# Eight slots for the first modulation weights, and the input's squares summed over tiles by TensorE

## The chip, the core and the metric

The kernel runs on one core of a Trainium2 chip. A core has TensorE (PE in the profile; its weight loads are PEld), VectorE (DVE), ScalarE (ACT) and GpSimd (POOL), and SyncE (SP), which here does nothing but issue transfers. The engines run their own instruction lists and meet only at semaphores. The metric is the device time of one execution in microseconds, less is better.

## The reference

The program computes two transformer blocks on one sequence of 512 tokens and 1024 features, in float32. What the change touches is the very first step of the first block:

```
mod = einsum('bd,de->be', silu(c), w_ada) + b_ada        # 1024 x 6144 weights
shift1, scale1, gate1, shift2, scale2, gate2 = split(mod, 6)
y    = x * rsqrt(mean(x * x, axis=-1) + eps)             # per token, over 1024 features
hmix = (y * g_norm1) * (1 + scale1) + shift1
proj = hmix @ w_in                                       # 1024 x 11264 weights
```

After it come stick-breaking attention, retention, a gated feed-forward layer, and the second block with a gated delta rule, a long convolution, cross attention and another feed-forward layer. Of all six parts of `mod` only `shift1` and `scale1` are needed before the first large product can start.

## The kernel before

Activations lie with features on the 128 partitions: `resid` is x as 8 tiles of 128 features by 512 tokens. Large products are done in three TensorE passes, on a high and a low part of each operand, so each weight unit (128 x 1024, 512 KB, tile `raw`) is split: ScalarE writes `w_hi` (`split_hi`), GpSimd then writes `w_lo` = raw - w_hi (`split_lo`, L449), and TensorE waits for both. There are 324 such units in a ring of four slots. Every engine's order is written out by hand, one function per engine, and no scheduler moves anything.

The opening stage, before the first large product, runs like this.

- SyncE issues the three constant tables, then 16 blocks of modulation weights (`ada0`, 512 KB each; blocks 0 to 7 give `shift1`, 8 to 15 `scale1`), with `resid` (2 MB) behind block 3, then the first weight units. `ada0` has four slots, so from block 4 on each issue waits until VectorE has used the block four places earlier (L382 to L386).
- VectorE multiplies each block by the activated conditioning vector and accumulates over 8 blocks in `adac0` (`ada`, L975 for a first block, L976 for the others). Between blocks 13 and 14 stands `invert()` (L981), the reciprocal of the norm's root, which waits for ScalarE's root. Behind block 15 stand the addition of the bias (L993), the gain (L995) and the normalised tiles (`tn` L1008, `x_lo` L1004).
- ScalarE squares the 8 tiles of `resid` (`square_tile`), the first into `sqacc`, the others into the two halves of `tn`; GpSimd adds each to `sqacc` (`add_square`, L436). ScalarE then waits for the sums over features, takes the root, and only then splits the first three weight units (`w_hi`).
- TensorE sums over the partitions by multiplying with a column of ones. `modulation` (L1683) does this for the 8 column blocks of `adac0`; `stat` (`column_sums`, L1655) does it for `sqacc`, in four matmuls of one output column each, and `spread_rs` (L1662) broadcasts the reciprocal root over the partitions. Its order here is: modulation of blocks 0 to 7, stat, spread, modulation of blocks 8 to 15, first large product.

The profile has two records for each of these float32 matmuls: the four of `stat` are eight rows of L1655.

Of the kernel before, what the change touches and what calls it, by code (L numbers as in the profile page):

```python
# [33 lines left out]
F32 = mybir.dt.float32  # L34
# [3 lines left out]
ACT = mybir.ActivationFunctionType  # L38
AX = mybir.AxisListType

P = 128
D = 1024
KT = D // P
T = 512
NB = T // P
EPS = 1e-6
UNIT = 1024
RING = 4
AHEAD = RING - 1

SB_DIM = 64
PAIRS = 8
# [117 lines left out]
T0, _ = starts(TILES)  # L170
# [29 lines left out]
def build_program(nc, dram):  # L200
    ctx = ExitStack()
    with ctx:
# [42 lines left out]
        over = at[0]  # L245

        def overlay(start, *specs):

            out, o = [], start
            for name, shape, dt in specs:  # L250
                t, o = put(name, shape, dt, where=o)
                out.append(t)
            assert o <= nc.sbuf_usable_end, (specs, o - nc.sbuf_usable_end)
            return out, o

        gate_t = tn

        (ada0, adac0), _ = overlay(over, ("ada0", (P, 4, UNIT), F32), ("adac0", (P, 2, UNIT), F32))


        qk_at = [norm_at, norm_at + T * 4, norm_at + 2 * T * 4, norm_at + 3 * T * 4]
# [67 lines left out]
        def sem(name):  # L329
# [6 lines left out]

            "dve_step", "act_step", "pool_step",
            "decay_free", "decay_loaded", "consts_loaded", "x_loaded", "tables_loaded", "consts_ready", "stored",
            "ada0_loaded0", "ada0_loaded1", "ada0_loaded2", "ada0_loaded3", "ada1_loaded", "ada_used",
            "ada_ready", "c_ready_act",  # L340
            "sq_ready", "stat_ready", "root_ready", "recip_ready", "rs_ready", "res_ready", "rsq_ready", "rsq_used",
            "hs_ready", "hrecip_ready", "glogit_ready", "tap_ready", "tap_used", "normed", "norm_hi", "x_ready",
# [22 lines left out]
        @block.sync  # L365
        def _(sp_):
            def load(u):
                s = u.slot(RING)
                if u.i is not None or u.c >= RING:

                    sp_.wait_ge(lo_ready, (u + (1 - RING)).val())
                if u.i is None:
                    src = dram["weights"][u.c]
                else:
                    src = dram["weights"][bass.ds(u.val(), 1), :, :].rearrange("a p n -> (a p) n")
                sp_.dma_start(raw[s][:], src).then_inc(raw_loaded[s], 16)

            sp_.dma_start(cols[:], dram["cols"]).then_inc(S["consts_loaded"], 16)
            sp_.dma_start(small[:], dram["small"]).then_inc(S["consts_loaded"], 16)
            sp_.dma_start(halves[:], dram["halves"]).then_inc(S["consts_loaded"], 16)  # L380
            for n in range(16):
                if n >= 4:  # L382
                    sp_.wait_ge(S["ada_used"], n - 3)
                sp_.dma_start(ada0[:, n % 4, :], dram["ada"][n]).then_inc(S[f"ada0_loaded{n % 4}"], 16)
                if n == 3:
                    sp_.dma_start(resid[:], dram["x"]).then_inc(S["x_loaded"], 16)  # L386
            for u in range(RING):
                load(At(u))
            def load_units(first, end):
                with sp_.Fori(0, (end - first) // 4) as i:  # L390
                    for j in range(4):
                        load(At(first + j, i, 4))

            load_units(RING, U0["sb_out"] + 4)

            sp_.wait_ge(S["osb_ready"], PAIRS)
            sp_.dma_start(angles[:], dram["tables"][:, 0:2 * T]).then_inc(S["tables_loaded"], 16)
            load_units(U0["sb_out"] + 4, U0["ret"])
            with sp_.Fori(0, RET_H) as i:
                for j in range(16):  # L400
                    if 6 <= j < 14:

                        n = At(2 * KT + j - 6, i, 8)
                        sp_.wait_ge(S["ada_used"], n.val())
                        sp_.dma_start(ada1[:], dram["ada"][bass.ds(n.val(), 1), :, :]
                                      .rearrange("a p n -> (a p) n")).then_inc(S["ada1_loaded"], 16)
                    load(At(U0["ret"] + j, i, 16))
                    if j == 3:

                        sp_.wait_ge(S["decay_free"], i + 1)  # L410
                        sp_.dma_start(decay[:], dram["tables"][:, bass.ds(i * T + 2 * T, T)]
                                      ).then_inc(S["decay_loaded"], 16)
            rest = U0["ret"] + 64
            load_units(rest, U0["mix_out"] + 4)

            sp_.wait_ge(S["gdn_over"], 1)
            sp_.wait_ge(S["x_ready"], X_MIX)
            sp_.dma_start(memf[:], dram["mem"]).then_inc(S["mem_loaded"], 16)
            load_units(U0["mix_out"] + 4, NU)

            for k in range(KT):
                sp_.wait_ge(S["resid_ready"], k + 1)
                sp_.dma_start(dram["out"][:, k, :], resid[:, k, :]).then_inc(S["stored"], 16)
            sp_.wait_ge(S["stored"], 16 * KT)


        @block.gpsimd
        def _(pool):
            step = Count(pool, S["pool_step"])
            rsq, used = Count(pool, S["rsq_ready"]), Count(pool, S["rsq_used"])  # L430

            def add_square(k):

                rsq.next()
                if k:
                    used.own(nc.gpsimd.tensor_tensor(sqacc[:], sqacc[:], tn[:, k % 2, :], ALU.add))  # L436
                if k == KT - 1:
                    pool.sem_inc(S["sq_ready"], 1)

            def add_squares():  # L440
                for k in range(KT):
                    add_square(k)

            add_squares()

            def split_lo(u):
                s = u.slot(RING)
                pool.wait_ge(hi_ready, (u + 1).val())
                nc.gpsimd.tensor_tensor(w_lo[s][:], raw[s][:], w_hi[s][:].bitcast(F32),  # L449
                                        ALU.subtract).then_inc(lo_ready, 1)  # L450

            def split_units(first, end):
                with pool.Fori(0, (end - first) // RING) as i:
                    for j in range(RING):
                        split_lo(At(first + j, i, RING))

            split_units(0, U0["gdn_in"])

            def next_phase(first, end):

                for j in range(AHEAD):
                    split_lo(At(first + j))
                add_squares()
                split_lo(At(first + AHEAD))
                split_units(first + RING, end)

            next_phase(U0["gdn_in"], U0["mix_out"])

            tap_used = Count(pool, S["tap_used"])
            for m, (n, j) in enumerate(POOL_TAPS):  # L470
                if j:
                    pool.wait_ge(S["tap_ready"], m + 1)
                    tap_used.own(nc.gpsimd.tensor_tensor(cfy[:, n, :], cfy[:, n, :], tn[:, tap_used.at.c % 2, :],  # L473
                                                         ALU.add))
            pool.sem_inc(S["cf_pool"], 1)
            split_units(U0["mix_out"], U0["kv"])
            for j in range(AHEAD):
                split_lo(At(U0["kv"] + j))
            for k in range(KT):
                split_lo(At(U0["kv"] + AHEAD + k))  # L480
                if k:
                    add_square(k - 1)
            split_lo(At(U0["kv"] + AHEAD + KT))
            add_square(KT - 1)
            split_units(U0["kv"] + AHEAD + KT + 1, U0["up"])
            next_phase(U0["up"], NU)
# [3 lines left out]
        def _(act):  # L490
# [27 lines left out]
            def square_tile(k):  # L518

                if k >= 3:  # L520
                    own["rsq_used"].next()
                own["rsq_ready"].own(f(tn[:, k % 2, :] if k else sqacc[:], resid[:, k, :], ACT.Square))
# [14 lines left out]
            own["c_ready_act"].own(f(c_act[:], cols[:, C0["c"]:C0["c"] + KT], ACT.Silu))  # L537
            act.wait_ge(S["x_loaded"], 16)
            for k in range(KT):
                square_tile(k)  # L540
            own["rsq_used"].next(2)
            own["consts_ready"].next(6)
            root(1.0 / D)
            for u in range(AHEAD):
# [391 lines left out]
        def _(dve):  # L936
# [34 lines left out]
            def ada(w, dst, k):  # L971

                c = c_act[:, k:k + 1]
                if k == 0:
                    return V.tensor_scalar(dst[:], w, c, None, ALU.mult)  # L975
                return V.scalar_tensor_tensor(dst[:], w, c, dst[:], ALU.mult, ALU.add)  # L976
# [7 lines left out]
            for m in range(2):  # L984
                for k in range(KT):
                    n = m * KT + k
                    dve.wait_ge(S[f"ada0_loaded{n % 4}"], 16 * (n // 4 + 1))
                    own["ada_used"].own(ada(ada0[:, n % 4, :], adac0[:, m, :], k))
                    if n == 2 * KT - 3:
                        invert()  # L990

            own["ada_ready"].next(2)
# [589 lines left out]
        def _(pe):  # L1582
# [101 lines left out]
                ins.then_inc(S["ada_ready"], 1)  # L1684

            pe.wait_ge(S["consts_loaded"], 48)
            own["ada_used"].next(KT)
            modulation(adac0[:, 0, :])
            stat()
            spread_rs()  # L1690
            own["ada_used"].next(KT)
            modulation(adac0[:, 1, :], 1)
# [591 lines left out]
```

## Time and profile before

| What | us |
|---|---|
| Three timed runs, median (lowest to highest) | 2405.63 (2405.4 to 2406.29) |
| Profiled execution, span | 2403.4 |
| First large product starts, in the profiled execution | 49.72 |
| TensorE busy | 2154.4 (90%) |
| VectorE busy | 1154.8 (48%) |
| ScalarE busy | 881.3 (37%) |
| GpSimd busy | 949.1 (39%) |

The page gives the profiled execution's time as its span, from the first instruction to the last; the timed runs are 2.2 us longer at the median, which is what lies around the span. In a row of the timeline stand the start, the duration, the engine, the line and operation, what it writes and reads, how many instructions are merged in the row, and in brackets how long the engine had been idle and who released it. A merged row's duration runs from the start of its first instruction to the end of its last. In the page's chain of waits the end of the program is followed back from instruction to instruction.

### The profile page before, as it was taken

The page shows a single profiled execution, that of the slowest core. Times are in us where ns is not written, and L with a number is a line of the kernel's source. Part 1 is how long each engine was busy: PE and PEld are TensorE (multiplying, and loading weights), DVE is VectorE, ACT ScalarE, POOL GpSimd, SP SyncE. Part 2 cuts the span into 40 slices and gives each one's busy share as a digit, 9 for nine tenths or more (in the row PEclk, how much of TensorE's full clock was granted, in tenths as well). Part 3 has the DMA queues.
Part 4 walks back from the last instruction along what each step waited for, and adds up shares of the span by engine and source line. Part 5 has one row for each costly group of instructions (what it writes and reads, how often), then busy time and mean ns, then how long its engine had stood idle before and what let it go on. Part 6 is the DMA issues. An engine that isn't in the chain of part 4 may idle for free.

```text
span 2403.4 us, 28555 instructions
## 1 busy us (share of the span) xinstructions
PE 2154.4 (90%) x10018; PEld 1750.0 (73%) x10018; DVE 1154.8 (48%) x1216; ACT 881.3 (37%) x1027; POOL 949.1 (39%) x426
## 2 busy tenths in 40 slices
PE   3999998999999998999998899667979878888997
PEld 3778877787877877888886677656768556666785
DVE  6054402354454555111113743897671478787613
ACT  3466632323232334444223444543342333333321
POOL 3321133243433343444444433664275134334441
PEclk9999999999999998999999999898899999999998
DMA  7211032342424222322231221000233012222331
GB/s 250 88 38 50 9 123 102 117 150 99 157 83 148 70 91 70 102 96 96 97 105 61 79 79 62 1 1 1 97 99 129 22 49 84 74 87 71 101 108 44
DMA packets 56225, 203.58 MB, mean 85 GB/s; under 512 B 6240, under 2 KB 6368, under 8 KB 55904
## 3 DMA queue, kind: packets, MB, share of 16 engines
q1 hardware_dynamic: 56160, 202.70, 25.0%
q8 instruction: 43, 0.70, 0.1%
q14 instruction: 22, 0.18, 0.0%
HBM read 200.57 MB, written 2.10 MB: 84 GB/s over the span
## 4 chain that ended last, share of the span: by engine, by line
PE 66%; DVE 24%; ACT 3%; issue 3%; DMA 1%; POOL 1%; DVEq 1%; SPq 0%; ACTq 0%; POOLq 0%
PE acc L1598 16%; PE acc L1600 16%; PE acc L1599 16%; DVE tn L1558 5%; DVE cfy L1344 2%; PE aux L1598 2%; PE aux L1599 2%; PE aux L1600 2%; DVE tn L1293 2%; DVE tn L1556 2%; PE acc L1801 1%; PE aux L1655 1%; DVE fin L958 1%; DMA ada<-in_ada 1%; PE acc L1712 1%
## 5 line engine op out<-in xcount | busy, mean ns | idle before, releaser
L449 POOL TENSOR_TENSOR w_lo<-raw,w_hi 128x1024 fp32r<-128x1024 f32 x324 | 801.4, 2480 | 1299.3 <-ACT w_hi L495 1298.5
L1598 PE MATMUL acc<-x_hi,w_hi 128*128 128x512 f32 x1544 | 621.6, 403 | 68.5 <-DVEq L946 52.7
L1600 PE MATMUL acc<-x_hi,w_lo 128*128 128x512 f32 x1544 | 608.5, 394 | 0.0
L1599 PE MATMUL acc<-x_lo,w_hi 128*128 128x512 f32 x1544 | 608.4, 394 | 0.0
L495 ACT ACTIVATE w_hi<-raw 128x1024 fp32r<-128x1024 f32 x324 | 339.8, 1059 | 608.7 <-PE acc L1600 489.0
L1598 PEld LDWEIGHTS acc<-x_hi,w_hi 128*128 128x128 f32 x1544 | 294.5, 191 | 159.2 <-issue 78.5
L1600 PEld LDWEIGHTS acc<-x_hi,w_lo 128*128 128x128 f32 x1544 | 293.9, 190 | 63.3
L1599 PEld LDWEIGHTS acc<-x_lo,w_hi 128*128 128x128 f32 x1544 | 294.8, 191 | 58.2
L495 ACT ACT_TABLE_LOAD x91 | 116.8, 1283 | 53.0 <-PE aux L1655 22.7
L1558 DVE SCALAR_TENSOR_TENSOR tn<-fin,cols,tn 128x512 f32<-128x512 f32 x88 | 128.3, 1458 | 13.1 <-DVE tn L1558 3.3
L473 POOL TENSOR_TENSOR cfy<-cfy,tn 128x512 f32<-128x512 f32 x70 | 99.5, 1421 | 72.3 <-ACT tn L495 68.9
L1205 DVE TENSOR_TENSOR ht<-acc,tn 128x512 f32<-128x512 f32 x22 | 15.2, 691 | 182.5 <-PE acc L1600 178.7
L976 DVE SCALAR_TENSOR_TENSOR adac<-ada,c_act,adac 128x1024 f32<-128x1024 f32 x42 | 61.9, 1474 | 68.7 <-DMA ada<-in_ada 67.4
L1598 PE MATMUL aux<-w_hi,x_hi 128*128 128x512 f32 x192 | 76.2, 397 | 6.5 <-DVE x_lo L1004 5.2
L1599 PE MATMUL aux<-w_lo,x_hi 128*128 128x512 f32 x192 | 75.9, 395 | 0.0
L1600 PE MATMUL aux<-w_hi,x_lo 128*128 128x512 f32 x192 | 75.7, 394 | 0.0
L1598 PE MATMUL acc<-g_hi,w_hi 128*128 128x512 f32 x176 | 69.8, 396 | 0.2 <-DVEq L946 0.2
L1599 PE MATMUL acc<-g_lo,w_hi 128*128 128x512 f32 x176 | 69.7, 396 | 0.0
L1599 PE MATMUL acc<-h_lo,w_hi 128*128 128x512 f32 x176 | 69.7, 396 | 0.0
L1598 PE MATMUL acc<-h_hi,w_hi 128*128 128x512 f32 x176 | 69.7, 396 | 0.0
L1600 PE MATMUL acc<-g_hi,w_lo 128*128 128x512 f32 x176 | 69.7, 396 | 0.0
L1600 PE MATMUL acc<-h_hi,w_lo 128*128 128x512 f32 x176 | 69.7, 396 | 0.0
(320 smaller groups left out, 3335.7 us busy)
## 6 DMA issues: line engine op xcount, KB each, us to landing
raw<-in_weights SPq DMA_DIRECT2D x324, 512.0 KB, 3.5
ada<-in_ada SPq DMA_DIRECT2D x48, 512.0 KB, 3.7
resid<-in_x SPq DMA_DIRECT2D x1, 2048.0 KB, 12.5
out<-resid SPq DMA_DIRECT2D x8, 256.0 KB, 2.0
decay<-in_tables SPq DMA_DIRECT2D x4, 256.0 KB, 3.5
memf<-in_mem SPq DMA_DIRECT2D x1, 1024.0 KB, 4.8
angles<-in_tables SPq DMA_DIRECT2D x1, 512.0 KB, 3.6
small<-in_small SPq DMA_DIRECT2D x1, 320.0 KB, 3.1
```

The source lines that it names most:

```text
L449: nc.gpsimd.tensor_tensor(w_lo[s][:], raw[s][:], w_hi[s][:].bitcast(F32), ALU.subtract).then_inc(lo_ready, 1)
L473: tap_used.own(nc.gpsimd.tensor_tensor(cfy[:, n, :], cfy[:, n, :], tn[:, tap_used.at.c % 2, :], ALU.add))
L495: return nc.scalar.activation(out, in_, func, **kw)
L958: (end or step).own(V.tensor_tensor(dst, bank(t), rs_sb, ALU.mult))
L976: return V.scalar_tensor_tensor(dst[:], w, c, dst[:], ALU.mult, ALU.add)
L1293: ins = V.scalar_tensor_tensor(y, x, w, y, ALU.mult, ALU.add)
L1344: step.own(V.scalar_tensor_tensor(y, x, w, y, ALU.mult, ALU.add))
L1556: ins = V.tensor_scalar(y, x, w, b, ALU.mult, ALU.add)
L1558: ins = V.scalar_tensor_tensor(y, x, w, y, ALU.mult, ALU.add)
L1598: M(out, a_hi, b_hi, start=first, stop=False)
L1599: M(out, a_hi, b_lo, start=False, stop=False)
L1600: return M(out, a_lo, b_hi, start=False, stop=last)
```

## The change

It does three things. The ring for the first 16 blocks of modulation weights has eight slots instead of four, so an issue waits for the block eight places earlier. ScalarE writes the 8 squared tiles to 8 tiles of a new buffer `sq0`, with no wait between them but for its own writes, and signals once, behind the last; GpSimd's seven additions in this stage are gone, and `stat` sums over all 8 tiles, with 32 matmuls in place of 4, and now stands ahead of the first modulation in TensorE's list. And `invert()` stands behind block 8 in VectorE's list, not behind block 13. Later norms keep the old scheme.

```
-        (ada0, adac0), _ = overlay(over, ("ada0", (P, 4, UNIT), F32), ("adac0", (P, 2, UNIT), F32))
+        (ada0, adac0, sq0), _ = overlay(over, ("ada0", (P, ADA_RING, UNIT), F32), ("adac0", (P, 2, UNIT), F32),
+                                        ("sq0", (P, KT, T), F32))
...
             for n in range(16):
-                if n >= 4:
-                    sp_.wait_ge(S["ada_used"], n - 3)
-                sp_.dma_start(ada0[:, n % 4, :], dram["ada"][n]).then_inc(S[f"ada0_loaded{n % 4}"], 16)
+                if n >= ADA_RING:
+                    sp_.wait_ge(S["ada_used"], n - ADA_RING + 1)
+                sp_.dma_start(ada0[:, n % ADA_RING, :], dram["ada"][n]).then_inc(S[f"ada0_loaded{n % ADA_RING}"], 16)
...
-            add_squares()
...
             act.wait_ge(S["x_loaded"], 16)
             for k in range(KT):
-                square_tile(k)
-            own["rsq_used"].next(2)
+                (step if k < KT - 1 else own["sq_ready"]).own(f(sq0[:, k, :], resid[:, k, :], ACT.Square))
...
-                    dve.wait_ge(S[f"ada0_loaded{n % 4}"], 16 * (n // 4 + 1))
-                    own["ada_used"].own(ada(ada0[:, n % 4, :], adac0[:, m, :], k))
-                    if n == 2 * KT - 3:
+                    dve.wait_ge(S[f"ada0_loaded{n % ADA_RING}"], 16 * (n // ADA_RING + 1))
+                    own["ada_used"].own(ada(ada0[:, n % ADA_RING, :], adac0[:, m, :], k))
+                    if n == KT:
                         invert()
...
             pe.wait_ge(S["consts_loaded"], 48)
+            own["sq_ready"].next()
+            stat([sq0[:, k, :] for k in range(KT)])
             own["ada_used"].next(KT)
             modulation(adac0[:, 0, :])
-            stat()
             spread_rs()
```

On TensorE, from the start of its list to the first matmuls of the large product, the order before is this (`adac_83` is the buffer `adac0`).

```order
L1581 UNCONDITIONAL_BRANCH
L1683 MATMUL aux<-small,adac_83 128x1 x8
L1655 MATMUL aux<-small,sqacc 128x1 x4
L1662 MATMUL aux<-small,rcol 128x128 x4
L1683 MATMUL aux<-small,adac_83 128x1 x8
```

The same place in the changed kernel, whose lines are one less here, and in which `sq_84` is `sq0`:

```order
L1580 UNCONDITIONAL_BRANCH
L1654 MATMUL aux<-small,sq_84 128x1 x32
L1682 MATMUL aux<-small,adac_83 128x1 x8
L1661 MATMUL aux<-small,rcol 128x128 x4
L1682 MATMUL aux<-small,adac_83 128x1 x8
```

The sum of squares has moved to the front and has eight times the matmuls.

On VectorE, from the first modulation block to the gain, before (`ada_82` is `ada0`):

```order
L975 TENSOR_SCALAR adac_83<-ada_82,c_act 128x1024
L976 SCALAR_TENSOR_TENSOR adac_83<-ada_82,c_act,adac_83 128x1024 x7
L975 TENSOR_SCALAR adac_83<-ada_82,c_act 128x1024
L976 SCALAR_TENSOR_TENSOR adac_83<-ada_82,c_act,adac_83 128x1024 x5
L981 RECIPROCAL rcol<-rcol 128x4
L976 SCALAR_TENSOR_TENSOR adac_83<-ada_82,c_act,adac_83 128x1024 x2
L993 TENSOR_TENSOR mod<-aux,cols 128x16
L995 SCALAR_TENSOR_TENSOR gain_67<-mod,cols 128x8
```

and in the changed kernel:

```order
L974 TENSOR_SCALAR adac_83<-ada_82,c_act 128x1024
L975 SCALAR_TENSOR_TENSOR adac_83<-ada_82,c_act,adac_83 128x1024 x7
L974 TENSOR_SCALAR adac_83<-ada_82,c_act 128x1024
L980 RECIPROCAL rcol<-rcol 128x4
L975 SCALAR_TENSOR_TENSOR adac_83<-ada_82,c_act,adac_83 128x1024 x7
L992 TENSOR_TENSOR mod<-aux,cols 128x16
L994 SCALAR_TENSOR_TENSOR gain_67<-mod,cols 128x8
```

The reciprocal has moved up by five blocks: seven blocks now stand behind it, where two stood.

## Rows read from the trace of the kernel before

**Rows 1.** The page's first line.

```profile
span 2403.4 us, 28555 instructions
```

**Rows 2.** Chain of waits, first 57 us: start, duration, engine and work.

```profile
19.26 2.18 DVE adac L976
...
34.14 5.42 DMA ada<-in_ada
...
39.65 1.30 DVE adac L976
...
40.99 3.59 PE aux L1683 x16
...
44.88 1.86 DVE gain L995
...
48.37 1.21 DVE x_lo L1004
...
49.72 0.77 PE aux L1598
```

**Rows 3.** Windows: stretch, busy time by engine, granted TensorE clock, DMA share, GB/s.

```profile
15.00:20.00 5.00, 0.00 (x0) 0.00 (x0) 2.02 (x2) 1.89 (x3) 1.91 (x1) 1.00 0.98 399
20.00:25.00 5.00, 0.00 (x0) 0.00 (x0) 4.93 (x3) 1.42 (x3) 4.76 (x4) 1.00 0.83 238
```

**Rows 4.** Timeline of ScalarE in the opening stage.

```profile
16.65 0.63 ACT L495 ACTIVATE sqacc<-resid 128x512 f32<-128x512 f32 x1 [11.30 <-DMA resid<-in_x]
17.32 1.29 ACT L495 ACTIVATE tn<-resid 128x512 f32<-128x512 f32 x2
...
36.40 0.26 ACT L495 ACTIVATE rcol<-aux,eps 128x4 f32<-128x4 f32 x1
40.92 1.06 ACT L495 ACTIVATE w_hi<-raw 128x1024 fp32r<-128x1024 f32 x1 [4.25 <-DMA raw<-in_weights]
```

**Rows 5.** Timeline of TensorE in the opening stage.

```profile
25.98 3.54 PE L1683 MATMUL aux<-small,adac 128*128 128x1 f32 x16 [25.98 <-DVE adac L976]
33.14 1.87 PE L1655 MATMUL aux<-small,sqacc 128*128 128x1 f32 x8 [3.62 <-POOLq L438]
```

**Rows 6.** Timeline of TensorE, column sums between large products, at 1420 us.

```profile
1420.51 3.63 PE L1655 MATMUL aux<-small,kdec 128*128 128x1 f32 x32
1423.99 6.46 PE L1655 MATMUL aux<-small,vb 128*128 128x1 f32 x32
```

**Rows 7.** Windows of TensorE alone, same place: busy, granted clock, DMA share, GB/s.

```profile
1424.00:1427.00 3.00, 3.00 (x19) 0.59 0.51 169
1427.00:1430.00 3.00, 3.00 (x16) 0.50 0.06 25
```

**Rows 8.** Timeline of VectorE in the opening stage.

```profile
9.23 3.93 DVE L976 SCALAR_TENSOR_TENSOR adac<-ada,c_act,adac 128x1024 f32<-128x1024 f32 x3 [0.50 <-DMA ada<-in_ada]
...
36.79 0.18 DVE L981 RECIPROCAL rcol<-rcol 128x4 f32<-128x4 f32 x1
```

**Rows 9.** Timeline of GpSimd in the opening stage.

```profile
18.09 14.94 POOL L436 TENSOR_TENSOR sqacc<-sqacc,tn 128x512 f32<-128x512 f32 x7 [17.64 <-ACT tn L495]
42.05 6.97 POOL L449 TENSOR_TENSOR w_lo<-raw,w_hi 128x1024 fp32r<-128x1024 f32 x3 [9.02 <-ACT w_hi L495]
```

**Rows 10.** Timeline of VectorE and GpSimd in the second feed-forward layer, 2210 to 2225 us.

```profile
2210.56 0.75 DVE L1558 SCALAR_TENSOR_TENSOR tn<-fin,cols,tn 128x512 f32<-128x512 f32 x1 [0.15 <-DVE tn L1558]
...
2219.18 5.20 POOL L449 TENSOR_TENSOR w_lo<-raw,w_hi 128x1024 fp32r<-128x1024 f32 x2 [9.32 <-ACT w_hi L495]
2219.32 2.81 DVE L1558 SCALAR_TENSOR_TENSOR tn<-fin,cols,tn 128x512 f32<-128x512 f32 x1 [0.15 <-DVE tn L1556]
2222.29 2.65 DVE L1558 SCALAR_TENSOR_TENSOR tn<-fin,cols,tn 128x512 f32<-128x512 f32 x1 [0.15 <-DVE tn L1558]
```

**Rows 11.** Chain of waits, within the first large product.

```profile
50.49 0.43 PE aux L1599
...
55.99 0.24 PE aux L1600
```

More of the change, by code:

```diff
@@ L49 @@
 AHEAD = RING - 1
+ADA_RING = 8
 SB_DIM = 64
@@ L338, in build_program @@
             "decay_free", "decay_loaded", "consts_loaded", "x_loaded", "tables_loaded", "consts_ready", "stored",
-            "ada0_loaded0", "ada0_loaded1", "ada0_loaded2", "ada0_loaded3", "ada1_loaded", "ada_used",
+            *[f"ada0_loaded{n}" for n in range(ADA_RING)], "ada1_loaded", "ada_used",
             "ada_ready", "c_ready_act",
```

## The prediction

> **What bounds the kernel now.** I read the page first. Its span is 2403.4 us [rows 1], and the edited code all lies ahead of the first large product at 49.72 us [rows 2]. From there on TensorE goes its old way with the old instructions, so the question is how far that start moves. The second view is the chain of waits over the opening stage [rows 2]. It runs through VectorE's accumulation of the modulation blocks (`adac`). Each of them takes 2.18 us on the chain while GpSimd adds squares, 1.30 without. It then waits 5.42 us for the transfer of the last block, does that block at 39.65, and goes through TensorE's second modulation (3.59), the gain (1.86), the first `x_lo` (1.21) and into the product. The windows, third, show why the transfer was late: with the queue full the DMA moved 399 GB/s, with four slots tied to the slow VectorE 238 [rows 3]. So before, both VectorE beside GpSimd and the ring of four bind. The timelines of the engines, fourth, give the durations below.
>
> **Part 1, the eight slots.** With eight slots the issues are never behind VectorE: up to block 7 they wait for nothing, and block 15 waits for block 7. The bytes up to block 15 are 16 x 0.52 MB, 2.1 MB of `resid` and 0.8 MB of tables, 11.3 MB; at 399 GB/s that is 28 us, and with the 2 us before the first bytes all blocks are there by about 31 us, against 39.6. The first weight unit follows about 1.3 us later and the fourth at about 36. `resid` stands at the same place in the queue, so it lands as before, about 16.6; blocks 4 to 7 now queue right behind it. If they shared its engines a little it would be late by up to one block (1.3 us); I take 0 and keep 1.3 for the range.
>
> **Part 2, the squares.** ScalarE starts at 16.65; one square has a pitch of 0.67 us (16.65 to 17.32), so the eighth ends at 16.65 + 7 x 0.67 + 0.63 = 22.0 [rows 4]. GpSimd's 14.94 us of additions [rows 9] go, and with them the 0.9 us that each one added to a VectorE instruction beside it. But TensorE now has 32 matmuls, 64 records, where it had 8 records. In this stage 8 records take 1.87 us and 16 take 3.54 [rows 5], which is 0.21 us a record. So 64 take 1.87 + 56 x 0.21 = 13.6 us, and the sums are ready at 22.0 + 0.1 + 13.6 = 35.7. Before, they were ready at 33.14 + 1.87 = 35.01 [rows 5]. All that ScalarE gained is spent on TensorE, and 0.7 us more.
>
> Would the clock rise during 13.6 us of work? The granted-clock column reads 1.00 in these first windows, but the durations say otherwise. At 1420 us the same column sums come in two groups of 32 records behind large products [rows 6]. The first takes 3.63 us (0.11 a record) and the second 6.46 (0.20). The granted clock is 0.59 and then 0.50 in the second, 1.2 GHz, though TensorE is busy in all of it [rows 7]. The 0.21 of the opening is thus the lower level, and a stream of one-column matmuls did not hold the upper one, still less does it reach it. I cost all 64 records low. The Trainium skill, page "TensorE: Matmul & The Clock Gate", section "Part 1: The HAM clock gate", has sustained matmul activity raise TensorE from its lower to its full clock. By that rule alone the stream would speed up on its way; the trace does not agree for matmuls of this shape. It is a rival below.
>
> **Part 3, the reciprocal behind block 8.** This is the step that decides. VectorE's list is strict: the reciprocal waits for ScalarE's root, the root for the sums, and blocks 9 to 15 stand behind it. From the end of the sums to the end of the reciprocal it was 36.97 - 35.01 = 1.96 us [rows 5, 8]. So VectorE, done with block 8 at about 24.5 us, stands idle until 35.7 + 1.96 = 37.7, with all the data there from 31 on. Then come seven blocks at 3.93 / 3 = 1.31 each [rows 8], 9.2 us. Before, two stood behind it, and they waited for a transfer.
>
> Nor do they run alone. ScalarE splits the first weight unit when the root is done. The unit has landed by then, so this is at 36.66 + 0.7 = 37.4 instead of 40.92 [rows 4], and GpSimd starts `w_lo` at about 38.5, three in a row (before: 42.05 to 49.02, rows 9). What does one cost a block? In the feed-forward layer a VectorE instruction of this kind takes 0.75 alone and 2.81 and 2.65 beside two `w_lo` [rows 10], so each adds 1.9 to 2.1. In the opening a block of 1.28 to 1.30 took 2.18 beside an addition of half `w_lo`'s width, 0.9 more [rows 2, 9], 1.8 for the full width. I take 2.0 for each of three, 6.0 (bounds 5.4 and 6.6; zero if they didn't meet, a rival). Block 15 ends at 37.7 + 9.2 + 6.0 = 52.9, against 40.95.
>
> **Part 4, what is given back.** From block 15 to the large product it was 49.72 - 40.95 = 8.8 us [rows 2]. The gain took 1.86 because it stood beside a `w_lo`; the nearest instruction of that size alone is the reciprocal, 0.18 [rows 8], and the three `w_lo` are now over by about 49. That gives 1.7. The first `x_lo` took 1.21 and takes 0.75 alone, as in rows 10: 0.45. The rest stays, 6.6. The modulations keep their 3.54: the first one and the broadcast lie in VectorE's seven blocks and cost nothing while these last 15 us.
>
> **Sum.** The product starts at 52.9 + 6.6 = 59.5, which is 9.8 us later. As a check by differences: reciprocal 0.7 later, five more blocks behind it 6.6, the transfer wait of 1.4 us ahead of block 15 gone, contention 6.0, given back 2.1, makes +9.8. Afterwards the first matmuls go at 0.43 us and from 55.99 on at 0.24 [rows 11], as the clock rises 6 us after the start; should that fall earlier or later against the new start, by 2.5 us at most, it is worth -1.2 to +0.3. Nothing behind it absorbs a later start, since from there the chain is TensorE's own. The span becomes 2413.2, and with the 2.2 us that the median of the timed runs lies above the span, 2415.4.
>
> **Rivals.**
> 1. The clock rises from the first sums on (ends on the other side, no change). All 64 records at 0.11 are 7.3 us, the sums end at 29.4 and the reciprocal at 31.4. `w_hi` then waits for the first weight unit (about 32) and meets the blocks all the same. Block 15 ends at 31.4 + 9.2 + 6.0 = 46.6, the product starts at 53.2: +3.5, or +1.7 if the last modulation is fast too. 2407.3 to 2409.1. It decides from a record time of about 0.13 on; for it speaks only the length of the stream, against it rows 6 and 7.
> 2. The clock rises part way, after some 6 us as in rows 11: 28 slow records and 36 fast, sums at 32.1, +6.2, 2411.8. Slower still.
> 3. GpSimd's `w_lo` and the blocks don't hinder each other: 9.8 - 6.0 = +3.8, 2409.4, no change. Against it the 2.18 of rows 2 and the 2.65 of rows 10.
> 4. The start comes sooner, because VectorE does not stand still. With all blocks used as they land it would end block 15 at about 33 and the product would start at 40, 10 us sooner, 2396. This is what the eight slots would give by themselves; it needs the root by about 25 us, and the sums alone take longer.
>
> **How the numbers follow.** The forecast's own mechanism has 0.80, rival 2 has 0.06, rival 1 has 0.06, rival 3 has 0.05 and rival 4 with everything unforeseen on that side 0.03. A measurement of this kernel can tell about 0.2% from no change, 4.8 us. The forecast and rival 2 are slower, 0.86; rivals 1 and 3 are no change, 0.11; faster 0.03. The range of the forecast itself is +8 (contention at its low bound, an early clock) to +12 (at its high one, a late `resid`). To leave out no more than 2 in 10 it is stretched down to rivals 2 and, in part, 3: 2410 to 2418.
>
> **What would show it.** Right: TensorE's sums over `sq0` as one block of 64 records from about 22 to 36 us; VectorE idle from about 24.5 to 37.7, released by the root; three blocks of over 3 us beside `w_lo` and four of 1.3; the gain in about 0.2; the large product from about 59.5. Wrong: sums that end before 33, blocks of 1.3 beside `w_lo`, or a span that moves by less than the start of the product does, which would mean slack behind it that I don't see.

## The result and the profile after

| | median us | lowest to highest | runs |
|---|---|---|---|
| before | 2406.24 | 2405.4 to 2407.14 | 6 |
| changed | 2412.71 | 2410.44 to 2417.24 | 6 |

The ratio is 1.003, with a 95% interval of 1.0018 to 1.0041: slower by 7.2 us, 4.3 to 9.9. The forecast was 2415.4, its range 2410 to 2418. The profiled execution of the changed kernel has a span of 2410.9 us and took 2412.76. Two of the later runs, one in experiment 1 (3072 us) and one in 9 (4062 us), showed a much lower granted clock than all others (0.66 and 0.85), and the ratios leave them out.

This is the chain of waits of the changed kernel, first 65 us: start, duration, engine and work. It answers to [rows 2].

```profile
21.43 13.80 PE aux L1654 x64
...
36.61 0.27 ACT rcol L495
...
36.98 0.19 DVE rcol L980
37.19 1.30 DVE adac L975
38.51 3.27 DVE adac L975
41.81 3.25 DVE adac L975
45.09 3.26 DVE adac L975
48.37 1.30 DVE adac L975
...
52.35 3.59 PE aux L1682 x16
...
56.24 0.18 DVE gain L994
...
58.05 0.76 DVE x_lo L1003
...
58.95 0.76 PE aux L1597
...
63.12 0.43 PE aux L1597
63.55 0.30 PE aux L1598
63.85 0.23 PE aux L1599
```

Before, this chain ran through transfers and blocks. Now it waits for TensorE's sums, then for the root, and only then come seven blocks. Three of these take 3.26 us instead of 1.30. The large product starts at 58.95, 9.2 us later than the 49.72 of [rows 2]. Its matmuls reach their fast pace at 63.85, 4.9 us after the start; before, that took 6.3 us (55.99, rows 11). The matmuls are the same, and at 65 us the changed kernel is 8.5 us late instead of 9.2.

The timelines of the other three engines, of the changed kernel, answer to [rows 4, 8, 9].

```profile
16.03 5.26 ACT L495 ACTIVATE sq<-resid 128x512 f32<-128x512 f32 x8 [9.99 <-DMA resid<-in_x]
35.32 1.28 ACT L495 ACT_TABLE_LOAD   x1 [14.03 <-PE aux L1654]
```

```profile
22.60 0.75 DVE L974 TENSOR_SCALAR adac<-ada,c_act 128x1024 f32<-128x1024 f32 x1
36.98 0.18 DVE L980 RECIPROCAL rcol<-rcol 128x4 f32<-128x4 f32 x1 [13.63 <-ACT rcol L495]
37.19 15.10 DVE L975 SCALAR_TENSOR_TENSOR adac<-ada,c_act,adac 128x1024 f32<-128x1024 f32 x7
```

```profile
38.05 9.21 POOL L449 TENSOR_TENSOR w_lo<-raw,w_hi 128x1024 fp32r<-128x1024 f32 x3 [37.59 <-ACT w_hi L495]
```

The squares are done at 21.3, but the sums only at 35.2 (forecast: 22.0 and 35.7; before, the sums were ready at 35.01). VectorE stands idle for 13.63 us, released by ScalarE's root. Of the 1.93 us from the end of the sums to the end of the reciprocal, ScalarE's load of a function table ahead of the root is 1.28. Then GpSimd's three `w_lo` take 9.21 us where they took 6.97 [rows 9]. With no blocks beside them, in experiment 4, they take 6.96, so both sides pay.

These are windows of the changed kernel, with busy time by engine as in [rows 3]. The transfers run at full rate from 10 to 35 us, here from 25 to 35 (before: 238 GB/s from 20 us on, rows 3).

```profile
25.00:30.00 5.00, 5.00 (x25) 5.00 (x25) 0.00 (x0) 0.00 (x0) 0.00 (x0) 1.00 1.03 412
30.00:35.00 5.00, 5.00 (x25) 5.00 (x25) 0.00 (x0) 0.00 (x0) 0.00 (x0) 1.00 1.00 397
```

So the eight slots did their work, and VectorE (third busy column, 0.00) used none of it. The clock column reads 1.00 here although the records have the pace of the low clock: before the first change of clock in this trace, the column can't be relied on.

### The profile page after: what moved, and what is told of

It is laid out like the page before. It is cut to its first block, busy times and chain, and to the rows that moved or that the text cites. A ratio compares the mean times of both kernels' runs of the same rounds, so it can differ in the third digit from the quotient of the medians.

```text
span 2410.9 us, 28738 instructions
## 1 busy us (share of the span) xinstructions
PE 2166.1 (90%) x10074; PEld 1761.9 (73%) x10074; DVE 1153.2 (48%) x1216; ACT 881.1 (37%) x1027; POOL 937.8 (39%) x419
## 4 chain that ended last, share of the span: by engine, by line
PE 67%; DVE 23%; ACT 3%; issue 3%; POOL 1%; DVEq 1%; DMA 1%; SPq 0%; ACTq 0%; POOLq 0%
PE acc L1597 17%; PE acc L1599 16%; PE acc L1598 16%; DVE tn L1557 5%; DVE cfy L1343 2%; PE aux L1597 2%; PE aux L1598 2%; PE aux L1599 2%; DVE tn L1292 2%; PE aux L1654 2%; DVE tn L1555 2%; PE acc L1801 1%; DVE fin L957 1%; PE aux L1742 1%; PE acc L1712 1%
```

## The experiments

Each was profiled once and timed in up to five rounds beside the kernel before. The kernel before scattered by 9 to 16 us from its lowest to its highest time in these later runs, so medians are told with their ratio's interval. "Start" is the first matmul of the large product in the profile. "Square" is the start of ScalarE's first square, which waits for `resid`: it varies by 1.2 us between profiles, and by half a us between the two of the kernel before (16.65 and 17.20). That scatter is part of every start, so the text also counts starts "from the square", the difference of the two columns.

| kernel | start | square | median | before | ratio (95%) |
|---|---|---|---|---|---|
| changed | 58.95 | 16.03 | 2412.71 | 2406.24 | 1.0030 (1.0018 to 1.0041) |
| reciprocal behind block 13 | 49.36 | 16.54 | 2403.99 | 2406.38 | 0.9985 (0.9974 to 0.9995) |
| eight slots alone | 48.79 | 16.79 | 2404.29 | 2406.38 | 0.9991 (0.9982 to 0.9999) |
| squares alone, four slots | 48.47 | 17.18 | 2404.38 | 2406.38 | 0.9987 (0.9978 to 0.9997) |
| weight split after block 15 | 55.80 | 16.56 | 2410.78 | 2406.38 | 1.0016 (1.0007 to 1.0025) |
| sums tile by tile | 54.63 | 16.25 | 2409.91 | 2405.90 | 1.0009 (0.9998 to 1.0019) |
| reordered | 42.03 | 16.11 | 2397.45 | 2405.90 | 0.9957 (0.9945 to 0.9970) |
| clock raised ahead | 58.50 | 16.77 | 2412.49 | 2405.90 | 1.0026 (1.0014 to 1.0037) |
| one tile summed | 42.68 | 16.72 | 2398.51 | 2405.90 | 0.9965 (0.9952 to 0.9978) |
| before, again | 50.59 | 17.20 | 2406.81 | 2407.24 | 0.9998 (0.9988 to 1.0007) |
| start delayed | 58.15 | 17.20 | 2414.70 | 2407.24 | 1.0031 (1.0019 to 1.0044) |
| reordered, four slots | 46.96 | 17.05 | 2401.89 | 2407.24 | 0.9976 (0.9966 to 0.9987) |

**1. The reciprocal put back behind block 13.**

```
-                    if n == KT:
+                    if n == 2 * KT - 3:
                         invert()
```

> The changed kernel with the reciprocal put back behind block 13 of VectorE's list; all else as changed. Theory A (the place of the reciprocal decides: it stalls VectorE with seven blocks behind it, which then run into three w_lo): the sums still end at about 35.2 us and the reciprocal at 37.2, but only blocks 14 and 15 follow, one of them beside a w_lo, so block 15 ends at about 41.8 (changed: 52.3) and the large product starts at about 49.2 (changed: 58.95, before: 49.72). Time about that of before, 2405 to 2407. Theory B (the 32 matmuls of the sum are what costs, wherever the reciprocal stands): the start stays above 56 us and the time at 2410 or more.

Chain of waits of this kernel:

```profile
21.95 13.80 PE aux L1654 x64
...
37.71 1.30 DVE adac L975
39.03 3.27 DVE adac L975
...
42.34 3.58 PE aux L1682 x16
...
46.23 0.60 DVE gain L994
...
49.36 0.77 PE aux L1597
```

The sums are as long, and as late from the square, and the loss is gone: theory A. The place of one short instruction in VectorE's list is worth 9.6 us of start, 10.1 from the square. The median is 2.4 us under that of the kernel before, 1 us below the 2405 to 2407 that I expected.

**2. Eight slots alone.** (The kernel before, with `ADA_RING = 8` as in the change.)

> The kernel before with eight slots and nothing else changed. Theory A (the transfer wait of 1.4 us before block 15 goes, but the first w_lo now meets block 15): block 15 ends at about 41.6, the last w_lo at about 46.3, the product starts at about 49, 0.5 to 1 us sooner than before; 2405 to 2406, no difference that can be measured. Theory B (the transfer wait was the bound and all blocks move forward): blocks 4 to 15 at the pace of the transfers, the product starts before 46 and the time falls by 4 us or more.

Chain of waits of this kernel:

```profile
32.08 2.18 DVE adac L977
...
37.14 1.30 DVE adac L977
38.46 3.27 DVE adac L977
```

Theory A. The wait of 5.42 us for the last transfer is gone from the chain, but block 15 meets the first `w_lo` instead: the early weights start GpSimd early. The blocks up to 34 us still take 2.18 us beside GpSimd's additions. Start 48.79, 0.9 us sooner (1.1 from the square); the time is barely shorter.

**3. Squares on TensorE alone, four slots, reciprocal behind block 13.**

```
-ADA_RING = 8
+ADA_RING = 4
```

(and the edit of 1.)

> The changed kernel with four slots and the reciprocal behind block 13: only the squares are moved to TensorE. Theory A (the root binds, the slots are worth nothing here): blocks 4 to 13 run in about 1.3 us each and are done before the root, and the product starts as in the kernel with eight slots and the reciprocal behind block 13, about 49.2. Theory B (four slots starve VectorE also without GpSimd beside it): block 13 is not done by 37 us and the product starts 1 us or more later than with eight slots.

Start 48.47, not later than with eight slots in experiment 1: 0.9 us sooner, and 1.5 from the square. Block 13 ends at 33.9 us (30.8 with eight), both before the root. With four slots the weights come later, the first `w_lo` starts at 40.3 and meets no block: blocks 14 and 15 take 2.60 us together against 4.58 in experiment 1. So theory A, with a twist that I had not foreseen: the slower ring kept the two engines apart. All this is with the reciprocal behind block 13; four slots with the reciprocal behind block 8 were not run.

**4. The first weights split only after block 15.** (ScalarE waits for block 15 between the root and the first `w_hi`, so the `w_lo` come later too.)

```
             root(1.0 / D)
+            act.wait_ge(S["ada_used"], 2 * KT)
             for u in range(AHEAD):
```

> The changed kernel, but ScalarE splits the first three weight units only after block 15, so that no w_lo runs beside blocks 9 to 15. Theory A (a w_lo holds up a VectorE instruction with two inputs in SBUF by 2 us): the seven blocks behind the reciprocal take 1.3 us each, 9.2 instead of 15.1; three w_lo then run from about 47.6 to 54.6 and meet the gain and the first x_lo, so the product starts at about 55.5, 3.5 us sooner than in the changed kernel. Theory B (the long blocks wait for something else): still 15 us for the seven, and the product starts at 60 or later since the w_lo come later.

Chain of waits of this kernel:

```profile
37.72 1.29 DVE adac L976
39.04 1.30 DVE adac L976
...
45.64 1.30 DVE adac L976
46.98 3.59 PE aux L1683 x16
...
50.87 1.96 DVE gain L995
...
54.46 1.20 DVE x_lo L1004
...
55.80 0.76 PE aux L1598
```

All seven blocks take 1.30 us, 9.2 together: the long blocks were the three `w_lo`, 5.9 us in all (forecast 6.0). The edit moves ScalarE's `w_hi` as well, but those are not the cause: in the changed kernel they ended at 39.86, and the second and third long blocks began after that. What waits for a `w_lo` now is the gain, 1.96 for a 128 x 8 instruction that took 0.18 in the changed kernel. GpSimd's timeline, 51 to 52 us, has the one beside it:

```profile
50.46 2.33 POOL L449 TENSOR_TENSOR w_lo<-raw,w_hi 128x1024 fp32r<-128x1024 f32 x1
```

The gain ends at 52.8, as this `w_lo` does.

**5. Sums begun at the first squared tile.** (ScalarE now signals each tile; the reciprocal stays behind block 8.)

```
-            own["sq_ready"].next()
-            stat([sq0[:, k, :] for k in range(KT)])
+            for k in range(KT):
+                own["sq_tile" if k < KT - 1 else "sq_ready"].next()
+                for b in range(NB):
+                    m = M(aux[:, 5 * T + b:5 * T + b + 1], sq0[:, k, b * P:(b + 1) * P], ones[:, 0:1], ...)
```

> The changed kernel, but TensorE waits for each squared tile by itself and begins its sums at the first, instead of waiting for all eight; the reciprocal stays behind block 8. Theory A (TensorE's 64 low-clock records bind, ScalarE's squares hide beside them): the sums run from about 16.9 to 30.6 us, the reciprocal ends at 32.6, block 15 at about 47.6 and the product starts at about 54.2, 4.7 us sooner than in the changed kernel. Theory B (the sums are paced by ScalarE or slowed by the waits between tiles): the sums end after 33 and less than 2.5 us is won.

The 64 records run from 17.02 to 30.8, 13.79 us as before, and the start is 54.63 (expected 54.2): TensorE binds, ScalarE's squares hide beside it. The time can no longer be told from that of the kernel before. This also shows that a 32-matmul sum need not cost its whole length.

**6. Reordered: 5, the reciprocal behind block 15, both modulations ahead of the spread.**

```
-                    if n == KT:
+                    if n == 2 * KT - 1:
                         invert()
...
             modulation(adac0[:, 0, :])
-            spread_rs()
             own["ada_used"].next(KT)
             modulation(adac0[:, 1, :], 1)
+            spread_rs()
```

> The changed kernel with the sums begun at the first squared tile, the reciprocal behind block 15 of VectorE's list, and TensorE's order: sums, first modulation, second modulation, spread. If the reading of the opening is right (slots worth having once nothing stalls VectorE), blocks 4 to 15 go at the pace of the transfers and end by about 33 us, the second modulation ends at about 37.6, the spread at about 39.6, and the product starts at 42.5 to 43, some 7 us sooner than before and 16 sooner than in the changed kernel: 2398 to 2400. Theory B (something behind the opening takes the gain): the product starts there but the time falls by less than 4 us.

Chain of waits of this kernel:

```profile
16.88 13.78 PE aux L1689 x64
30.66 6.83 PE aux L1682 x32
37.49 1.93 PE aux L1661 x8
...
42.03 0.76 PE aux L1597
```

VectorE does blocks 9 to 15 in 9.21 us from 23.80 on, 1.32 us a block, with no wait between them. The start is at 42.03 and the time is 2397.45, both about half a us under what I expected. That is 8.4 us below the kernel before at the median, 10.3 by the ratio (7.2 to 13.2): this version beats both. From the end of the first square, 16.9, to 39.4 the chain is TensorE alone, 104 short records at the low clock. Three edits were made at once; what each is worth is not separated here.

**7. Needless large matmuls ahead of the sums.**

```
+            for n in range(15):
+                M(acc[:, 0:T], ident, small[:, 0:T], start=True, stop=True)
             own["sq_ready"].next()
             stat([sq0[:, k, :] for k in range(KT)])
```

> The changed kernel with 15 needless float32 matmuls of 512 columns on TensorE ahead of the sums, so that its clock is up when they begin. Theory A (the record of 0.21 us is the low clock's, and a stream of one-column matmuls does not hold the clock): the first records take 0.11 us, then the granted clock falls within the stream as it did at 1424 us, and the rest take 0.21; the 64 take 7 to 11 us instead of 13.8, and the product starts at 52.5 to 56. Theory B (0.21 is what such a matmul costs in the opening, whatever the clock, say from the transfers beside it): still 13.8 and a start at 59 or later.

TensorE's timeline and, below it, windows of TensorE (busy, granted clock, DMA share, GB/s) in this kernel:

```profile
5.33 15.30 PE L1687 MATMUL acc<-small 128*128 128x512 f32 x30 [5.33 <-DMA halves<-in_halves]
22.08 12.69 PE L1654 MATMUL aux<-small,sq 128*128 128x1 f32 x64 [1.45 <-ACT sq L495]
```

```profile
22.10:23.30 1.20, 1.20 (x11) 1.00 1.00 399
24.00:26.00 2.00, 2.00 (x11) 0.50 1.03 412
```

Eleven records in 1.20 us while the clock is granted in full, eleven in 2.00 at 0.50 (1.2 GHz), with the same transfers beside them (each count takes in records that the window cuts). That refutes theory B: 0.21 us is the low clock's price. But the clock fell only 1.3 us into the stream, so 12.69 us and the start of 58.50 miss theory A's numbers (7 to 11, and 52.5 to 56); how soon it is lost I had wrong. TensorE had been idle for 1.45 us before the stream, which may have had its part in the fall. In [rows 7] it was busy throughout, and the clock fell all the same. Nor did the stream raise the clock again in its remaining 11.4 us.

**8. Only one tile summed.**

```
-            stat([sq0[:, k, :] for k in range(KT)])
+            stat([sq0[:, 0, :]])
```

> The changed kernel with the sum taken over the first squared tile only, 4 matmuls instead of 32 (this leaves out seven eighths of the sum of squares). Theory A (the late root alone stalls VectorE): the sums end at about 24 us, the reciprocal at 26, all blocks go at the pace of the transfers and end by about 33, and the product starts at 41 to 43 even with the reciprocal behind block 8. Theory B (the blocks would be held up anyway, by the transfers or by w_lo): block 15 ends after 38.

VectorE's timeline in this kernel:

```profile
25.73 0.18 DVE L980 RECIPROCAL rcol<-rcol 128x4 f32<-128x4 f32 x1 [1.68 <-ACT rcol L495]
25.94 9.21 DVE L975 SCALAR_TENSOR_TENSOR adac<-ada,c_act,adac 128x1024 f32<-128x1024 f32 x7
```

This kernel leaves out seven eighths of the sum. With the root early the same place behind block 8 costs a stall of 1.68 us, not 13.63. Block 15 ends at 35.1 (2 us later than I had it, since seven blocks follow the reciprocal back to back), the start is 42.68: theory A. So it takes both, the long sums and the early place of the reciprocal.

**9 and 10. The kernel before once more, and the kernel before with nothing but a later start.**

```
+            for n in range(34):
+                M(acc[:, 0:1], ident, ones[:, 0:1], start=True, stop=True)
             token_tiles(At(0), (0, 1, 2, 3), ready=own["x_ready"])
```

> The kernel before once more, unchanged, profiled a second time. Theory A (the timed runs and single profiles differ by where the clock's low stretches fall, the opening does not): the product starts within 1 us of 49.72, the span may differ by up to 3 us, and the ratio is 1. Theory B (the first profile of the kernel before was short or long in its opening, so that every shift read against it is off): the start differs by 1.5 us or more.

> The kernel before with 34 needless one-column matmuls on TensorE behind the second modulation, which hold it for 14.3 us from 44.6 us on: nothing but a later start of the product, at about 58.9. Theory A (nothing behind the opening absorbs a later start): the time rises by 9.2 us as the start does, less or more by where the clock's low stretches fall, 2413 to 2417. Theory B (there is slack of about 2 us behind the start, as the measured +7 for a start 9.2 later suggests): the rise is 7 us or less, and PE runs over the same 2 us sooner at one fixed place.

The second profile of the kernel before starts its product at 50.59 and has a span of 2405.9 (first: 49.72 and 2403.4), both within theory A. Its chain of waits:

```profile
54.35 0.43 PE aux L1600
...
55.04 0.23 PE aux L1599
```

Its matmuls are fast 4.5 us after the start; in the first profile that took 6.3. So its later start is gone again at once: matmul by matmul, the two stand level at 65 us. The 2.5 us between their spans arise later.

The delayed kernel starts at 58.15, 7.6 us after that second profile and 8.4 after the first, and takes 7.5 us more at the median (ratio's interval 4.6 to 10.6). Its span is 7.9 us above the first profile's and 5.4 above the second's. So a later start is paid in full within what can be measured, though a slack of 2 us would also fit that interval. The start was 0.7 us sooner than I had it, and the time is inside the expected 2413 to 2417.

How two profiles can differ by 2 us in the same work shows in one stretch. These are windows of TensorE (busy, granted clock, DMA share, GB/s), at 919 us in the first profile of the kernel before, and 8 us later, at the same work, in the changed one:

```profile
919.00:933.00 14.00, 9.44 (x29) 0.51 0.01 2
```

```profile
927.00:941.00 14.00, 9.62 (x40) 0.76 0.00 1
```

The clock was low through the whole of it in the first and through half of it in the second. Compared matmul by matmul with that first profile, counted from the end, the changed kernel is 8.5 us late at 65 us, 8.2 at 800 us, 5.4 at 940 and 7.5 at 1440; the delayed kernel goes 8.3, 8.2, 5.7 and 7.9. Between the low stretches the lag stands still: the changed kernel's is 8.2 from 420 to 800 us and 6.2 to 6.3 from 1000 to 1290. So no place there absorbs the late start, and what comes and goes is where the clock falls. Between 113 and 119 us the second profile of the kernel before has its clock at 0.50 where the first has it at 1.00.

**11. The reordered kernel with four slots.** (The edits of 6 with `ADA_RING = 4`.)

> The reordered kernel (sums begun at the first squared tile, reciprocal behind block 15, both modulations ahead of the spread) with four slots instead of eight. Theory A (the slots bind once nothing else stalls VectorE): block 13 ends at about 33.9 as in the four-slot kernel of the first study, block 15 at 36.5 to 37.5, the second modulation ends at about 41 and the product starts at 44.5 to 46, some 3 us later than with eight slots. Theory B (TensorE's sums and modulations bind, the slots are worth nothing): the start stays within 0.7 us of 42.0.

VectorE's timeline in this kernel:

```profile
34.28 1.28 DVE L975 SCALAR_TENSOR_TENSOR adac<-ada,c_act,adac 128x1024 f32<-128x1024 f32 x1 [0.91 <-DMA ada<-in_ada]
36.91 1.28 DVE L975 SCALAR_TENSOR_TENSOR adac<-ada,c_act,adac 128x1024 f32<-128x1024 f32 x1 [1.34 <-DMA ada<-in_ada]
...
42.14 1.83 DVE L994 SCALAR_TENSOR_TENSOR gain<-mod,cols 128x8 f32<-128x8 f32 x1
```

Block 15 ends at 38.2 instead of 33.0, and the start is 46.96, 4.9 us later than with eight slots, 4.0 from the square (I had said 3: the gain and the first `x_lo` collide with the later `w_lo` too). Here the slots are worth 4.4 us of time at the median, between 2397.45 and 2401.89.

## Why the prediction was right

- **Part 1, the slots.** The transfers ran at 397 to 412 GB/s (399 taken). `resid` was not late, so that bound of the range was not needed. That they bring next to nothing while VectorE waits for the root, and much once it does not, is shown by 1 to 3 against 6 and 11. Four slots in the changed order itself were not run.
- **Part 2, the squares.** 64 records took 13.80 us (13.6 forecast); they ended at 35.2 (35.7), since the squares began at 16.03 instead of 16.65. That they run at the low clock is shown by 7. The rivals with a rising clock fall. By the rule of the Trainium skill ("TensorE: Matmul & The Clock Gate", "Part 1: The HAM clock gate") 13.8 us of sustained matmuls should have raised it; no run here agrees for one-column matmuls, neither this one nor the delayed kernel with its 68 records in 14.64 us.
- **Part 3, the reciprocal.** VectorE's stall, the seven blocks and the three `w_lo` came as worked out: block 15 ended at 52.3 (52.9). Shown by 1 (place), 4 (contention) and 8 (length of the sums). Rival 3 falls with 4.
- **Part 4, given back.** The gain took 0.18 and the first `x_lo` 0.76; 6.6 us from block 15 to the product, as forecast.
- **Sum.** The start moved 9.2 us against 9.8; counted from the square it moved 9.9 against the first profile of the kernel before and 9.5 against the second. Against their medians the time rose by 6.5 us, by the ratio 7.2, and the forecast time was 2.7 us too high. Of this 0.6 is the earlier landing of `resid`, which is scatter, and about 0.7 is the clock, which rose 4.9 us after the start and not 6.3. My range allowed 1.2 for that, but no row showed its bound of 2.5 us: in 4 the clock had risen 2.9 us after the start, 3.4 sooner than in rows 11. The rest is within the interval of the ratio and the scatter from the clock's low stretches; it is not attributed further. How much of a later start reaches the time depends on where these stretches fall, which the forecast could not know.
- **The sign of slack.** I had named a span that moves by less than the start as a sign of being wrong, and it did: 7.5 us against 9.2. The clock's rise is 0.7 of it, and the rest comes at the low stretches, as the comparison in 10 shows. My reason there was loose, since only 66% of the chain on the page of the kernel before is TensorE's and 24% is VectorE's. What held is that no place was found that absorbs the delay.
- **Rival 4** was the instructive one: its 2396 is nearly what the kernel reaches once the wait on the root is not ahead of the blocks (2397.45 in 6, with the sums begun early and both modulations ahead of the spread).

## What to carry to other kernels

In a list that an engine works off strictly, a wait costs what stands behind it: put it behind everything that does not need it, and ask how late its releaser really is, not how short the instruction is. In an opening without large products, work moved from an elementwise engine to one-column matmuls is moved to a TensorE at its low clock, here 0.21 us a record. A deeper ring shows nothing while something else stalls its reader, and may even start the next stage's work where it collides; judge it again after the stall is gone. And compare starts from the same event: here the landing of one transfer alone shifted them by up to 1.2 us.

## What the runs showed of the hardware that I had not expected

- TensorE at its full clock lost it 1.3 us into a stream of one-column matmuls after 1.45 us of idling (7), though it was busy in every record after that.
- A GpSimd `w_lo` of 128 x 1024 and a VectorE instruction with both inputs in SBUF hold each other up: a block of 1.30 us takes 3.26 beside a `w_lo`, three `w_lo` take 9.21 instead of 6.97, and even a 128 x 8 gain takes 1.96 us in 4 and 2.26 in the second profile of the kernel before, ending when the `w_lo` beside it ends. The `tn` instructions of the opening, whose second tensor is in PSUM, kept their 0.76 beside the same `w_lo`.
- The same kernel's low-clock stretches move from run to run: the two profiles of the kernel before are level at 65 us and 2.5 apart at the end. The first rise of the clock came 2.9 to 6.3 us after the start of the large product.
